# Two stacked transformer blocks on one core: the pooled stage as product, then a constant band

## What is computed

```python
def ada_modulation(c, w, b):
    mod = jax.nn.silu(c) @ w + b
    shift, scale, gate = jnp.split(mod, 3, axis=-1)
...
def multiscale_pool_mixer(h, pool_w, pool_scale):
    # windows 2, 4, 8, 16, one for each group of 256 features
    ...
        cnt = jnp.minimum(t + 1, w)
        pooled = (csg - lag) / cnt - hf[..., lo:hi]     # running mean minus the token itself
        outs.append(pooled.astype(h.dtype) @ pool_w[gi])
    return jnp.concatenate(outs, axis=-1) * pool_scale
...
    h = rms_norm(x, norm_w[layer, 0]) * (1.0 + scale) + shift
    y = multiscale_pool_mixer(h, ...)
    x = x + gate * y
    ...
    x = x + gate * (jnp.square(relu(h @ w1)) @ w2)
```

## Time and profile before

| | |
|---|---|
| median of 3 runs | 956.2 us (955.88 to 959.43) |
| the profiled execution, own time | 958.09 us |
| its span on the core | 956.4 us |
| granted TensorE clock, mean | 0.97 |
| HBM | 205 GB/s over the span |

### The profile page before, as it was taken

One profiled execution on the slowest core, in us unless ns is written; L12 is line 12 of the kernel. 1 busy time (PEld: TensorE's weight loads), 2 busy tenths in 40 slices (PEclk: granted clock), 3 DMA queues, 4 the chain that ended last, 5 costly groups with the idle time before them and its releaser, 6 DMA issues.

```text
span 956.4 us, 17671 instructions
## 1 busy us (share of the span) xinstructions
PE 888.4 (93%) x7028; PEld 852.6 (89%) x7028; DVE 692.1 (72%) x877; ACT 456.8 (48%) x573; POOL 58.0 (6%) x104
## 2 busy tenths in 40 slices
PE   2599999899999996799999999999999999999996
PEld 1388879799999996699999999988989999999996
DVE  4889878788878888766666556855487877776665
ACT  2347464566643333456663433444465444444445
POOL 2110110211111110000000000000000000000000
PEclk9789999999999996799999999999999999999998
DMA  9895755499989994057765555653435555654531
GB/s 336 300 339 193 244 200 177 130 319 322 317 306 330 330 316 134 23 184 234 239 199 176 175 183 168 197 166 130 157 90 177 177 179 187 218 173 158 169 126 44
DMA packets 156600, 196.60 MB, mean 206 GB/s; under 512 B 5341, under 2 KB 143116, under 8 KB 156556
## 3 DMA queue, kind: packets, MB, share of 16 engines
q1 hardware_dynamic: 142732, 145.64, 47.6%
q0 software_dynamic: 13824, 50.34, 14.4%
HBM read 194.90 MB, written 1.06 MB: 205 GB/s over the span
## 4 chain that ended last, share of the span: by engine, by line
PE 81%; DVE 9%; ACT 4%; issue 2%; DMA 2%; SPq 1%; DVEq 0%; ACTq 0%
PE G L557 15%; PE G L558 15%; PE G L559 15%; PE A L557 7%; PE A L559 7%; PE A L558 7%; DVE w_lo L1123 2%; ACT w_hi L1786 2%; PE G L632 2%; PE A L685 2%; PE G L633 2%; PE G L634 2%; DMA sinks<-in_attn_sinks_dram 1%; DMA MIX<-bias_rows 1%; DVE HN L1285 1%
## 5 line engine op out<-in xcount | busy, mean ns | idle before, releaser
L1123 DVE TENSOR_TENSOR w_lo<-raw,w_hi 128x2048 fp32r<-128x2048 f32 x135 | 307.1, 2275 | 163.7 <-ACT w_hi L1786 163.5
L1786 ACT ACTIVATE w_hi<-raw 128x2048 fp32r<-128x2048 f32 x135 | 256.6, 1901 | 265.7 <-PE A L559 132.4
L557 PE MATMUL G<-h_hi,w_hi 128*128 128x256 f32 x880 | 257.9, 293 | 22.5 <-DVE h_lo L1268 13.0
L558 PE MATMUL G<-h_lo,w_hi 128*128 128x256 f32 x880 | 253.3, 288 | 0.0
L559 PE MATMUL G<-h_hi,w_lo 128*128 128x256 f32 x880 | 253.2, 288 | 0.0
L557 PEld LDWEIGHTS G<-h_hi,w_hi 128*128 128x128 f32 x880 | 173.0, 197 | 29.5 <-issue 22.5
L558 PEld LDWEIGHTS G<-h_lo,w_hi 128*128 128x128 f32 x880 | 173.6, 197 | 0.2 <-issue 0.2
L559 PEld LDWEIGHTS G<-h_hi,w_lo 128*128 128x128 f32 x880 | 173.2, 197 | 0.0
L557 PE MATMUL A<-u_hi,w_hi 128*128 128x256 f32 x512 | 143.4, 280 | 0.7 <-DVE w_lo L1123 0.7
L558 PE MATMUL A<-u_lo,w_hi 128*128 128x256 f32 x512 | 142.9, 279 | 0.0
L559 PE MATMUL A<-u_hi,w_lo 128*128 128x256 f32 x512 | 142.9, 279 | 0.0
(11 more groups left out here) (325 smaller groups left out, 1315.7 us busy)
## 6 DMA issues: line engine op xcount, KB each, us to landing
raw<-in_mlp_w_dram SPq DMA_DIRECT2D x64, 1024.0 KB, 5.5
ada_raw<-in_ada_w_dram POOLq DMA_DIRECT2D x88, 512.0 KB, 5.7
raw<-in_w_in_dram SPq DMA_DIRECT2D x14, 1024.0 KB, 5.0
raw<-in_w_up_dram SPq DMA_DIRECT2D x11, 1024.0 KB, 5.4
raw<-in_w_gate_dram SPq DMA_DIRECT2D x11, 1024.0 KB, 5.3
raw<-in_attn_w_in_dram SPq DMA_DIRECT2D x9, 1024.0 KB, 7.1
raw<-in_w_down_dram SPq DMA_DIRECT2D x8, 1024.0 KB, 5.2
raw<-in_attn_w_out_dram SPq DMA_DIRECT2D x4, 1024.0 KB, 5.4
```

What stands on the lines that cost most here:

```text
L557: pe.matmul(dst, wh, ah, start=start, stop=False)
L558: pe.matmul(dst, wh, al, start=False, stop=False)
L1123: dve.tensor_tensor(w_lo[n % 2][:, 0:k, :], raw[n % RAW][:, 0:k, :], w_hi[n % 2][:, 0:k, :].bitcast(F32), ALU.subtract).then_inc(lo_done, 1)
L1786: act.activation(w_hi[n % 2][:, 0:k, :], raw[n % RAW][:, 0:k, :], ACT.Copy).then_inc(hi_done, 1)
```

## The change

The product with the pool weights comes first. Its input is X times the norm's gain alone, split in the passes of the first MLP's down product (`h_hi`, `h_lo`), so it starts without waiting for the root. Tokens now lie on the partitions of the result. VectorE multiplies it by the token's root and adds a row that carries the shift (the shift's column sums over the pool weights, `sw`), and writes `z_tok`; TensorE multiplies that by a band matrix (window mean minus identity), which VectorE builds from constants in the down passes 0, 1, 2 (one, one, two bands, six instructions each). The row of squares of n2 becomes a column (`token_sums`, `token_root`).

The modulation sums: gate1, scale2 and shift2 are turned by 24 transposes through the free G banks between up and down; gate2, scale3 and shift3 by 24 in the pooled stage. ScalarE adds the rows of all but gate1 (`rows_along`: four ACTIVATEs of 128x128 with an accumulator for each half), VectorE those of gate1. The sums' weights are worked off 2, 2, 2, 0 a pass of the first up product, not 2, 1, 2, 1, and in the last down pass two of them come before the residuals. The products' counters U shift by 6 and 10. SP loads block 49 only when `sw`'s inputs have been read out of the pool block.

```diff
-U_POOL, U_UP, ... = 29, (13, 33), ...
+U_POOL, U_UP, ... = 35, (13, 43), ...
+U_SUMS = 29
...
# SP
                     if layer == 0:
                         load(N_POOL, w_pool)
+                        for j in range(3):
+                            load(N_UP[1] + j, w_up1[1][:, :, j * COLS:(j + 1) * COLS])
+                        sp.wait_ge(sw_ready, 1)
...
# TensorE
+            def turned_free(m, part, u, blocks):
+                pe.wait_ge(ada_used, blocks)
+                for half in range(2):
+                    g_empty(u + half)
+                    for t in range(4):
+                        at = (4 * half + t) * P
+                        last = pe.transpose(G[(u + half) % 4][:, t * P:(t + 1) * P],
+                                            sums_of(m, part)[:, part, at:at + P], ident)
+                    last.then_inc(sums_turned, 1)
...
             up(0)
-            add_sums(1, "gate", ADA_D - 2)
+            for n, (m, part) in enumerate(((1, GATE), (2, SCALE), (2, SHIFT))):
+                turned_free(m, part, U_SUMS + 2 * n, ADA_D)
             down(0)
-            add_sums(2, "scale", ADA_D)
-            mean_square(2)
-            add_sums(2, "shift", ADA_D)
-            add_sums(2, "gate", ADA_E)
...
+            def pool_group(g):
+                pe.wait_ge(e2_ready, 2 * g + 2)
+                for k in range(2):
...
+                    for t in (2 * g, 2 * g + 1):
+                        pe.matmul(dst, h_hi[:, t, toks], w_hi[N_POOL % 2][:, t, :], start=t == 2 * g, stop=False)
+                        pe.matmul(dst, h_hi[:, t, toks], w_lo[N_POOL % 2][:, t, :], start=False, stop=False)
+                        last = pe.matmul(dst, h_lo[:, t, toks], w_hi[N_POOL % 2][:, t, :], start=False,
+                                         stop=t % 2 == 1)
+            pool_group(0)
+            pool_group(1).then_inc(pool_done, 1)
+            pool_group(2)
+            token_sums("ms2", 2)
+            pe.wait_ge(sw_ready, 1)
+            for p in range(2):
...
+                bank_done(f"sw{p}", pe.matmul(halves(dst), ones[:, :], HN[p][:, :, :], start=True, stop=True))
+            turn_sums(2, "gate", ADA_E)
+            pool_group(3).then_inc(block_used, 1)
+            turn_sums(3, "scale", ADA_E)
             for g in range(4):
...
+                if g == 2:
+                    turn_sums(3, "shift", ADA_E)
...
+                    pe.matmul(dst[:, 0:P + POOL_PAD], z_tok[:, 0, cols], band[:, g, :], start=True, stop=False,
+                              skip_group_check=True)
+                    last = pe.matmul(dst[:, P:S], z_tok[:, 1, cols], band2[g], start=False, stop=True,
+                                     skip_group_check=True)
+                last.then_inc(band_done, 1)
-            scale_and_shift(3)
             dst = bank_empty(pe, "ms3")
...
# VectorE, mlp(0)
-                        for _ in range((2, 1, 2, 1)[j] if with_ada else 0):
+                        for _ in range((2, 2, 2, 0)[j] if with_ada else 0):
                             ada_pair(0, done, i)
...
                 if layer == 0:
-                    part(1, "gate")
+                    for half in range(2):
+                        u = U_SUMS + half
+                        dve.wait_ge(sums_turned, half + 1)
+                        ins = dve.tensor_reduce(part_sums[:, 4 * half:4 * half + 4],
+                                                G[u % 4][:, :].rearrange("p (t k) -> p t k", t=4), AX_X, ALU.add)
+                        ins.then_inc(g_free[u % 4], 1)
...
+                    for u in range(U_SUMS + 2, U_SUMS + 6):
+                        dve.wait_ge(g_free[u % 4], u // 4 + 1)
+                    chain(with_bias(6 * DT, 2 * DT, 0))
+                    chain(factor(2))
...
+                def band_of(g):
+                    v, head = C[:, C_DIST:C_DIST + P + POOL_PAD], band[:, g, 0:POOL_PAD]
+                    chain(dve.tensor_scalar(band[:, g, :], v, ...))
+                    chain(dve.scalar_tensor_tensor(out=band[:, g, :], in0=v, ...))
+                    chain(dve.tensor_tensor(band2[g], band[:, g, 0:P], ident, ALU.subtract))
+                    chain(dve.scalar_tensor_tensor(out=head, in0=v[:, 0:POOL_PAD], ...))
+                    chain(dve.scalar_tensor_tensor(out=head, in0=v[:, 0:POOL_PAD], ...))
+                    dve.tensor_tensor(band[:, g, 0:P], band[:, g, 0:P], ident, ALU.subtract)
+                def out_tiles(i, last, bands=()):
...
                         if j < 3:
                             split_lo(n + 2, i)
-                        for _ in range((2, 2, 0, 0)[j] if with_ada else 0):
+                        if j == 2:
+                            for g in bands:
+                                band_of(g)
+                        if j == 2 and last:
+                            dve.wait_ge(sw_part, 1)
+                            for g in range(4):
...
+                                ins = dve.scalar_tensor_tensor(out=part, in0=raw[N_POOL % RAW][:, at, :], ...)
+                            ins.then_inc(sw_ready, 1)
+                        for _ in range((2, 2, 2 if last else 0, 0)[j] if with_ada else 0):
                             ada_pair(1, done, i)
                             done += 1
                     for m in range(2):
                         residual_tile(layer, n, 0, m, MOD[:, 1 + 2 * layer, 2 * DT:], i)
-                    if layer:
...
+                    for m in range(2):
+                        dve.wait_ge(e5_hi if layer else e2_hi, i * 2 + (m + 1))
...
+                if layer == 0:
+                    for i, bands in enumerate(((0,), (1,), (2, 3), ())):
+                        out_tiles(i, i == 3, bands)
...
# VectorE, pooled stage: the norms, windows and low parts of L1553 to L1591 go
+            for p in range(2):
...
+                    dve.scalar_tensor_tensor(out=z_tok[:, k, 512 * p:512 * p + 512], in0=G[u % 4][:, :],
+                                             scalar=t_rstd[:, k:k + 1], in1=sw[:, p, :], op0=ALU.mult,
+                                             op1=ALU.add).then_inc(g_free[u % 4], 1)
...
# ScalarE
+            def rows_along(bank, col):
+                for t in range(4):
+                    tile = bank[:, t * P:(t + 1) * P]
+                    ins = act.activation(tile, tile, ACT.Copy,
+                                         accum_out=mod_sums[:, col + t:col + t + 1])
+                return ins
...
+                if layer == 0:
+                    for n, col in ((2, DT), (4, 0)):
+                        for half in range(2):
+                            u = U_SUMS + n + half
+                            act.wait_ge(sums_turned, n + half + 1)
+                            rows_along(G[u % 4], col + 4 * half).then_inc(g_free[u % 4], 1)
...
             mlp(0)
-            root(2)
-            bank_was_read(act, "shift2")
+            token_root("ms2", t_rstd)
+            for p in range(2):
+                src = bank_full(act, f"sw{p}")
+                bank_read(f"sw{p}", act.activation(sw[:, p, :], src[:, :], ACT.Copy))
+            for name, col in (("gate2", 0), ("scale3", 2 * DT), ("shift3", DT)):
+                for half in range(2):
+                    src = bank_full(act, f"{name}{'ab'[half]}")
+                    bank_read(f"{name}{'ab'[half]}", rows_along(src, col + 4 * half))
```

More of the change, by code:

```diff
@@ L1102, in _ @@
                 if ks[0] == 0:
[L1103 to L1109 removed]
+                    token_sums("ms7", 7)
             turn_rows(3)
@@ new lines, in out_tiles @@
+                    split_lo(n + 2, i)
+                    for _ in range(6 - done if with_ada else 0):
+                        ada_pair(1, done, i)
+                        done += 1
+                if layer == 0:
+                    for i, bands in enumerate(((0,), (1,), (2, 3), ())):
+                        out_tiles(i, i == 3, bands)
+                else:
+                    with dve.Fori(0, 4) as i:
+                        out_tiles(i, False)
+                    chain.looped, chain.count = 0, start + 8
@@ L2022, in mlp @@
+                        if j == 2 and last:
+                            act.wait_ge(raw_full[N_POOL % RAW], 16 * (N_POOL // RAW + 1))
+                            for g in range(4):
+                                ins = act.activation(HN[g // 2][:, g % 2, :], raw[N_POOL % RAW][:, 2 * g, :],
+                                                     ACT.Copy, scale=MOD[:, 2, 2 * g:2 * g + 1])
+                            ins.then_inc(sw_part, 1)
                         split_hi(N_DOWN[layer] + j + 2, i)
+                with act.Fori(0, 4 if layer else 3) as i:
+                    out_tiles(i, False)
```

230 lines of the change are left out of this document (113 added, 117 removed).

## The result

| | before | after |
|---|---|---|
| median, 7 runs each, side by side | 958.08 us (955.73 to 959.68) | 963.23 us (958.53 to 964.32) |
| ratio, 95% interval | | 1.0051 [1.0029, 1.0074] |
| profiled execution: own time, span | 958.09, 956.4 us | 958.53, 956.8 us |

The changed kernel is slower by 0.5%. Its profiled execution is the shortest of its seven, so this profile shows 0.4 us of a loss of 5. Run again beside other runs of before, with a second profile, it took 960.95 against 958.59 (1.0032 [1.0021, 1.0043]); that profile (span 959.2) is the more typical one and is used beside the first.

The account below looks back on a forecast made before the run. TensorE, busy 93% of the span, was taken as the bound, with VectorE's chain ending the pooled stage. Terms -14.5 + 4.9 + 0.6 + 6.4 = -2.6 took the median from 956.2 to 953.6 us, range 945 to 962.

Parts of the forecast that it names:

- B: Pooled stage: TensorE's clock stays at half, gain 3 instead of 14.5, so 965 us; chance 0.13.
- Term 1: Pooled stage: the new order ends the last squares (ms3) earlier, at 381.5 instead of 397.2; -14.5 us after handoffs.
- Rival C: ScalarE's row sums don't overlap, 0.46 each instead of 0.28: +4.3, total 957.9 us; chance 0.14.
- Term 2: Boundary between up and down: 24 transposes through the G banks delay down, +4.9 us, plus 0.6 for the clock.
- Term 3: Down passes: four bands ahead of the residuals make w_lo and the next w_hi late, +6.4 us.
- Term 4: Costs nothing: 2, 2, 2, 0 order, DMA waits, SP's later loads, POOL's clearing, ScalarE's shift products, TensorE's pool matmuls.

Follow-up runs that it names:

- small transfers: Kernel before, modulation-row transfers in the first down layer bringing only 256 of 1024 columns: 957.8 us, 1.0001.
- the kernel with one band: Changed kernel with one band left in the first pass of the down layer and the three others at the boundary: 956.8 us, 0.9991.
- sums behind: Changed kernel with the 96 bytes of mod_sums moved behind the bands, so u_hi and f_hi lie where they lay before: 959.8 us, 1.0009.
- after, small loads: Changed kernel, modulation-row transfers in the first down layer bringing only 256 of 1024 columns: 958.2 us, 1.0002.
- bands spread: Changed kernel with one band in each pass of the first down layer instead of 1, 1, 2, 0: 963.0 us, 1.0053.
- four repairs: Changed kernel: mod_sums behind bands, shift sums in free banks, all bands at the boundary, unused 32 and 96 bytes ahead of e_hi and gate_ps: 945.3 us, 0.9869.
- after, again: Changed kernel run once more without edit, for a second profile: 961.0 us, 1.0032.

## Why the prediction was wrong

It said 953.6 in 945 to 962; 963.2 came, 9.6 more. Of that, 1.9 is the base: the kernel before had a median of 956.2 in the three runs that the prediction started from, and 958.1 in the seven beside the changed one. The change itself was forecast at -2.6 and measured at +5.1, and at +2.4 when it was run again. A loss of over 0.5% had a chance of 0.18 there, and B had most of it.

- **Term 1, the pooled stage (-14.5): right.** 24.7 us from the end of down to up, 24 forecast, row sums at 0.28: -15.0 in the first profile, -13.1 in the second. Rival C fell with the 0.28. The Trainium skill (VectorE: DVE Perf Modes, TRN2 errata) says that many small tiles pay the fixed cost each. The trace agrees with that much: four row sums of 128 columns out of PSUM take 4 x 0.28, where one copy of 512 columns out of PSUM takes 0.60 (ACTIVATE into sw, 383.42). What fell was my step from there to a read that doesn't overlap. B, the clock: 1.00 in the first profile until 390, but in the second it falls behind the 1.2 us wait for the squares and takes 1.7. I had weighed B as all or nothing, "once TensorE loses more than 7.4 us"; a small form of it came behind that wait in eight of the ten later profiles with the new stage.
- **Term 2, the boundary (+4.9 and 0.6): mechanism right,** 6.6 and 7.2 us where 6.75 was forecast. The loss measured +5.1 and +6.5, the second with a granted clock of 0.76 from 274 to 281. That VectorE idles there for 8 us followed from my own working (ScalarE's "next w_hi is due 5.6 after") and would have told me where bands are free.
- **Term 3, the passes (+6.4): failed, at +10.4 and +9.0,** and not in the part that it priced. With rows in time the bands cost 6.7: 1.4 each where I had 1.6, and 4.0 for two at once where I had 3.2, since TensorE's idling of 2.1 was followed by 1.7 of lost clock. The two errors offset each other, so that 6.7 is near 6.4 is partly luck. So is the length of a band: the numbers that I added give 1.7, not 1.6, and it took 1.56 because its first instruction took 0.23 and not 0.31. The step that failed is the one that let term 3 count bands alone, "with the losses below the data is there in time" (said in term 1). VectorE waited 7.1 to 7.5 us for rows, where it had waited 3.4, and that is 1.2 of the second profile's 9.0 and 2.6 of the first one's 10.4. The other 1.1 is the beat of 5.69.
- **Term 4, "costs nothing": wrong in two entries, and that is most of the miss.** The order 2, 2, 2, 0 in the up passes did cost nothing (every up block 5.76 as before). Two others did cost (their share within the passes is in term 3 already). "TensorE's 48 pool matmuls are as many as before" let me stop looking at matmuls that didn't change: 96 bytes put in front of them cost 2.4 us in the kernel before, and 2.2 by the ratios in the changed one. And "a DMA wait as the 1.34 fits in" was true in before, where small transfers change nothing, and false once the cover went: 2.9 us by the ratios in the changed kernel, 6.3 with the bands out of the way. These two make 5.1 of the 5.0 by which the repeated measurement misses -2.6. That they fill it to 0.1 is chance, since the boundary and the clock were off as well. What makes the first set of runs 2.7 longer still, no run shows.
- **The skill's figure in term 3.** The Trainium skill (same page and section) has 58 cycles plus the columns, 0.19 us for 128; the bands' rows have 0.29. The same section says that this row of its table comes out too low and gives 151 cycles plus the columns for an fp32 tensor_tensor, an estimated 0.29, which the rows match.
- **The range:** its top was C with a late boundary, a case that didn't come; no case held two losses that nobody had priced.

## What to carry to other kernels

When a change moves work into an engine's last slack, price what that slack was hiding too. Transfers that cost nothing before came to light here, and a row that came 2.3 us late cost 1.6 once a band stood behind it. An idle stretch of TensorE can cost more than itself: 1.7 of clock behind 2.1 in one profile, nothing behind 2.2 in another. Put constants where the engine waits anyway; here all four bands fit into a gap that the same change had opened. And compare where the tiles lie before and after any edit that adds one: a block that "didn't change" and takes 5.69 instead of 5.60 is the sign.

## What the runs showed of the hardware

- The cadence of fp32r matmuls of 256 columns was 0.1167 to 0.1200 us at a granted clock of 1.00, a block of 48 of them 5.60 to 5.76, and it changed with the places of tiles in SBUF alone: the kernel before took 0.9929 to 1.0026 of its time. At fixed places it was 5.69 and 5.76 in one layer of the kernel with one band.
- The clock fell behind some idle stretches of TensorE and not behind others as long. In the down passes it fell behind 1.79 (sums behind: 0.58 in the 4 us after), 2.14 (after, small loads: 0.83 over 10 us) and 3.17 (after: 0.73 over 6 us), and stayed at 1.00 behind 2.24 (after) and 2.22 (bands spread), and behind every one of 0.8 and less. At the boundary it stayed at 1.00 behind 3.62 (four repairs). Before the fp32 matmuls of the pooled stage it fell behind 1.22 (after, again) and not behind 1.00 (after).
- ACTIVATE with accumulator read on 128x128 out of PSUM: 0.28 each in a row of 16. Vector instructions with two inputs took 0.29 for 128 columns and 0.17 to 0.18 for 16, with 0.03 between them.
